# Three weight units of the first expert get places outside the ring

## What is computed

```python
logits = h @ w_router + b_router;  probs = softmax(logits, axis=-1)
vals, idx = lax.top_k(swapaxes(probs, 1, 2), 32)      # each expert takes 32 tokens
xe = h[idx]                                           # [16, 32, 1024]
a = einsum('becd,edf->becf', xe, w_gate_e)            # w_gate_e [16, 1024, 2048]
u = einsum('becd,edf->becf', xe, w_up_e)              # w_up_e   [16, 1024, 2048]
y = einsum('becf,efd->becd', silu(a) * u, w_down_e)   # w_down_e [16, 2048, 1024]
out = scatter_add(y * vals)
```

## Time and profile before

| | |
|---|---|
| median of three runs | 2342.8 us (2338.36 to 2347.49) |
| the profiled execution | 2340.59 us |
| its span, first to last instruction | 2338.8 us |
| mean granted TensorE clock | 0.871 |
| TensorE busy | 1814.7 us (78%) |
| VectorE, ScalarE busy | 830.5 us (36%), 632.7 us (27%) |
| moved by the DMA engines | 613.55 MB, 262 GB/s in the mean |

### The profile page before, as it was taken

The page is one execution under the profiler, slowest core; times in us unless marked ns, Lnnn a source line. Parts: engine busy times, 40 slices in busy tenths (PEclk is TensorE's granted clock), DMA queues, the critical chain, the costliest instruction groups (busy, mean ns, idle before and its releaser), DMA issues.

```text
span 2338.8 us, 33822 instructions
## 1 busy us (share of the span) xinstructions
PE 1814.7 (78%) x13686; PEld 1330.1 (57%) x13686; DVE 830.5 (36%) x1687; ACT 632.7 (27%) x1107; POOL 60.7 (3%) x94
## 2 busy tenths in 40 slices
PE   6999866656555556566555999969989997998998
PEld 4789721111111111111113989869979987988996
DVE  2364520000000000000004367754655544665553
ACT  1334300000000000000002256534633332643332
POOL 2000000000000000000000000100100000000000
PEclk7999978777888887877787899988989998998999
DMA  9886479999999999999997253243164543143540
GB/s 352 292 289 244 189 300 418 418 418 418 418 418 417 418 418 418 418 418 418 418 418 279 73 181 122 78 163 112 28 208 145 181 155 127 49 145 121 185 182 28
DMA packets 193908, 613.55 MB, mean 262 GB/s; under 512 B 8772, under 2 KB 62082, under 8 KB 161024
## 3 DMA queue, kind: packets, MB, share of 16 engines
q1 hardware_dynamic: 189856, 604.46, 67.1%
q0 software_dynamic: 3200, 7.14, 1.0%
q10 hardware_dynamic: 736, 0.38, 0.1%
HBM read 610.85 MB, written 5.03 MB: 263 GB/s over the span
## 4 chain that ended last, share of the span: by engine, by line
PE 52%; DMA 36%; DVE 4%; SPq 2%; issue 2%; DVEq 2%; ACT 1%; POOL 0%; POOLq 0%; ACTq 0%
PE psum L1247 51%; DMA ring<-in_w_down_e 18%; DMA ring<-in_w_up_e 17%; PE psum L1551 1%; DMA ring<-in_w_in 1%; SPq L696 1%; DVEq L1730 1%; DVE ring_r L646 1%; DVE xR L1712 0%; SPq L749 0%; DVEq L1713 0%; DVE xR L1714 0%; ACT arena L951 0%; PE psum L1327 0%; DVE mt L1725 0%
## 5 line engine op out<-in xcount | busy, mean ns | idle before, releaser
L1247 PE MATMUL psum<-ring,arena 128*32 128x512 f32 (+1 forms) x4316 | 544.1, 648 | 326.8 <-DMA ring<-in_w_up_e 135.9
L1247 PE MATMUL psum<-xR,ring_r 128*128 128x256 f32 x4416 | 576.6, 290 | 10.0 <-DVE xR L1714 7.0
L1247 PEld LDWEIGHTS psum<-xR,ring_r 128*128 128x128 f32 x4416 | 552.1, 196 | 22.3 <-issue 12.1
L1247 PEld LDWEIGHTS psum<-ring,arena 128*32 128x32 f32 x4316 | 155.5, 134 | 681.2 <-issue 225.6
L646 DVE TENSOR_TENSOR ring_r<-ring,ring_r 128x1024 fp32r<-128x1024 f32 (+2 forms) x332 | 377.3, 1171 | 280.3 <-ACT ring_r L637 280.0
L637 ACT CAST ring_r<-ring 128x1024 fp32r<-128x1024 f32 (+2 forms) x332 | 319.6, 1005 | 510.3 <-PE psum L1247 487.4
L1247 PE MATMUL psum<-arena 128*128 128x64 f32 (+8 forms) x1346 | 208.7, 363 | 21.1 <-ACT arena L1060 7.8
L1247 PE MATMUL psum<-ring_r,xR 128*128 128x256 f32 (+3 forms) x1488 | 208.8, 298 | 12.2 <-DVE xR L1714 9.9
L1247 PEld LDWEIGHTS psum<-ring_r,xR 128*128 128x128 f32 x1488 | 197.3, 208 | 17.7 <-DVE xR L1714 11.8
L1932 DVE TENSOR_TENSOR arena<-arena,psum 128x512 f32<-128x512 f32 x16 | 11.0, 687 | 493.1 <-PE psum L1247 493.1
L1247 PEld LDWEIGHTS psum<-arena 128*128 128x128 f32 (+5 forms) x1346 | 142.2, 185 | 56.8 <-issue 31.3
(11 more groups left out here) (199 smaller groups left out, 990.5 us busy)
## 6 DMA issues: line engine op xcount, KB each, us to landing
ring<-in_w_up_e SPq DMA_DIRECT2D x64, 2048.0 KB, 25.6
ring<-in_w_gate_e SPq DMA_DIRECT2D x64, 2048.0 KB, 23.7
ring<-in_w_down_e SPq DMA_DIRECT2D x64, 2048.0 KB, 26.9
ring<-in_w_in SPq DMA_DIRECT2D x30, 2048.0 KB, 11.9
ring<-in_w_ada SPq DMA_DIRECT2D x12, 2048.0 KB, 9.5
ring<-in_w_gate SPq DMA_DIRECT2D x22, 1024.0 KB, 5.4
ring<-in_w_up SPq DMA_DIRECT2D x22, 1024.0 KB, 8.1
ring<-in_w_down SPq DMA_DIRECT2D x10, 2048.0 KB, 7.9
```

The lines of the kernel that those rows point to most:

```text
L1247: return nc.tensor.matmul(o, l, r, start=s, stop=e)
```

## The change

Nine units of expert 0 are loaded before the experts begin, six in the ring as before and three outside: units 6 and 7 at the top of `arena` and unit 8 in the buffer `xR`. The two in `arena` are issued between the ring's third and fourth load, after waits for `z_done` and for two small stores of GpSimd that read tiles there; the one in `xR` is issued after the sixth. Unit 9 of expert 0 then goes to place 0, and all later units rotate from there (unit i to place (i - 3) mod 6). TensorE runs expert 0 written out and experts 1 to 15 in the loop; SyncE's loop runs over experts 1 to 14. For room, `wr` and `brow` stand below the top of the arena, the router's tiles overlie tiles of the expert loop, and GpSimd clears the second block's tiles only when nine units are used. The sum over all units, and what is computed, stays the same. Cut to its core:

```diff
+AHEAD = 3
-        xR = ctx.enter_context(nc.sbuf_tensor("xR", [P, 2 * KT * T], F32R))[:, :].rearrange("p (c k t) -> p c k t", c=2, k=KT)
+        x_moe, xR = twice("xR", 2 * KT * T)
+        xR = xR.rearrange("p (c k t) -> p c k t", c=2, k=KT)
...
-        wr = pl(KT * 32).rearrange("p (k e) -> p k e", k=KT)
-        brow = pl(NE)
+        top = Place(ARENA - KT * 32 - NE)
+        wr = top(KT * 32).rearrange("p (k e) -> p k e", k=KT)
+        brow = top(NE)
...
+        ahead_at = ARENA - KT * 32 - NE - 2 * SLOT
+        assert pm.at <= ahead_at
+        e_ahead = [arena[:, ahead_at:ahead_at + SLOT], arena[:, ahead_at + SLOT:ahead_at + 2 * SLOT], x_moe]
...
+        def moe_slot(e, i):
+            return (i if type(e) is int and e == 0 and i < RINGM else i - AHEAD) % RINGM
...
-            for i in [(N_MOE + j) % RING for j in range(RING)] + [RING]:
+            free = [(N_MOE + j) % RING for j in range(RING)]
+            for i in free + [RING]:
                 prev = max(n for n in range(N_MOE) if n % RING == i) if i < RING else N_MOE - 1
+                if i == free[3]:
+                    sp.wait_ge(z_done, 4)
+                    sp.wait_ge(rel_st, 16)
+                    sp.wait_ge(rel_na, 16 * 9)
+                    ahead_unit(0)
+                    ahead_unit(1)
                 sp.wait_ge(g_ready, LAST[prev] + 1)
-                expert_unit(0, i)
-            with sp.Fori(0, NE - 1) as e:
-                for i in range(RINGM, UPE):
-                    sp.wait_ge(e_unit, e * UPE + (i - RINGM + 1))
-                    expert_unit(e, i)
...
+                ring_unit(0, i)
+            ahead_unit(2)
...
+            for i in range(RINGM + AHEAD, UPE + AHEAD):
+                sp.wait_ge(e_unit, i - RINGM - AHEAD + 1)
+                ring_unit(i // UPE, i % UPE)
+            with sp.Fori(1, NE - 1) as e:
+                ring_units(e, AHEAD, UPE)
...
                 if n < RING:
-                    sp.wait_ge(e_unit, (NE - 1) * UPE + RINGM + n + 1)
+                    last = max(i for i in range(UPE) if moe_slot(1, i) == n)
+                    sp.wait_ge(e_unit, (NE - 1) * UPE + last + 1)
...
             pool.wait_ge(e_sel, 1)
+            pool.wait_ge(e_unit, RINGM + AHEAD)
...
-                pe.wait_ge(wm_ready[i % RINGM], e * (16 * UPE // RINGM) + 16 * (i // RINGM + 1))
-            with pe.Fori(0, NE) as e:
+                if type(e) is int and RINGM <= i < RINGM + AHEAD:
+                    pe.wait_ge(wx_ready[i - RINGM], 16)
+                    return e_ahead[i - RINGM]
...
+            expert(0)
+            with pe.Fori(1, NE) as e:
+                expert(e)
```

More of the change, by code:

```diff
@@ L348, in program @@
         csil = pl(KT * 32).rearrange("p (k n) -> p k n", k=KT)
-        wr = pl(KT * 32).rearrange("p (k e) -> p k e", k=KT)
-        brow = pl(NE)
+        top = Place(ARENA - KT * 32 - NE)
+        wr = top(KT * 32).rearrange("p (k e) -> p k e", k=KT)
+        brow = top(NE)
+        assert pl.at <= ARENA - KT * 32 - NE
         early = Place(ga_at)
@@ L370, in program @@
         xeT = pm(KT * CAP).rearrange("p (k c) -> p k c", k=KT)
+        routing = Place(pm.at)
         hT = pm(4 * P).rearrange("p (s n) -> p s n", s=4)
@@ L373, in program @@
         gu = pm(512)
+        lgp = routing(T)
+        work = routing(T)
+        mk = routing(T)
+        cnt = routing(T)
+        lg = routing(TT * NE).rearrange("p (t e) -> p t e", t=TT)
+        ex = routing(TT * NE).rearrange("p (t e) -> p t e", t=TT)
+        top8 = routing(8)
+        assert routing.at <= pm.at
         ysb = pm(T)
-        lgp = pm(T)
-        lg = pm(TT * NE).rearrange("p (t e) -> p t e", t=TT)
-        ex = pm(TT * NE).rearrange("p (t e) -> p t e", t=TT)
         prob = pm(TT * NE).rearrange("p (t e) -> p t e", t=TT)
[L379 to L382, removed]
         pp = pm((NE + 1) * 4).rearrange("p (e t c) -> p e t c", e=NE + 1, t=TT)
         cur = pm(4)
+        ahead_at = ARENA - KT * 32 - NE - 2 * SLOT
+        assert pm.at <= ahead_at
+        e_ahead = [arena[:, ahead_at:ahead_at + SLOT], arena[:, ahead_at + SLOT:ahead_at + 2 * SLOT], x_moe]
         p2 = Place(D)
@@ L485, in program @@
         wm_ready = [sem(f"wm_ready{i}") for i in range(RINGM)]
+        wx_ready = [sem(f"wx_ready{i}") for i in range(AHEAD)]
         w2_ready = [sem(f"w2_ready{i}") for i in range(RING)]
@@ L739, in _, with expert_unit @@
             wd = a["w_down_e"].rearrange("l e (k p) d -> p (l e k) d", p=P)
-            def expert_unit(e, i):
+            def expert_unit(e, i, d, landed_):
                 if i < 8:
@@ L744, in expert_unit @@
                     src = w[:, bass.ds(e * KT + 2 * (i % 4), 2), :]
-                    d = slot(i, RINGM).rearrange("p (k c) -> p k c", k=2)
+                    d = d.rearrange("p (k c) -> p k c", k=2)
                 else:
                     src = wd[:, bass.ds(e * (FE // P) + 4 * (i - 8), 4), :]
-                    d = slot(i, RINGM).rearrange("p (k c) -> p k c", k=4)
-                sp.dma_start(d, src).then_inc(wm_ready[i % RINGM], 16)
-            for i in [(N_MOE + j) % RING for j in range(RING)] + [RING]:
-                prev = max(n for n in range(N_MOE) if n % RING == i) if i < RING else N_MOE - 1
+                    d = d.rearrange("p (k c) -> p k c", k=4)
@@ new lines, in expert_unit, with ring_unit, ahead_unit @@
+                sp.dma_start(d, src).then_inc(landed_, 16)
+            def ring_unit(e, i):
+                n = moe_slot(e, i)
+                expert_unit(e, i, slot(n, RINGM), wm_ready[n])
+            def ahead_unit(j):
+                expert_unit(0, RINGM + j, e_ahead[j], wx_ready[j])
+            free = [(N_MOE + j) % RING for j in range(RING)]
+            for i in free + [RING]:
+                prev = max(n for n in range(N_MOE) if n % RING == i) if i < RING else N_MOE - 1
+                if i == free[3]:
[4 more added lines that the diff above has]
+                    ahead_unit(1)
@@ L754, in _, with ring_units @@
                 sp.wait_ge(g_ready, LAST[prev] + 1)
-                expert_unit(0, i)
-            with sp.Fori(0, NE - 1) as e:
-                for i in range(RINGM, UPE):
+                ring_unit(0, i)
+            ahead_unit(2)
+            def ring_units(e, lo, hi):
+                for i in range(lo, hi):
                     sp.wait_ge(e_unit, e * UPE + (i - RINGM + 1))
-                    expert_unit(e, i)
-                for i in range(RINGM):
-                    sp.wait_ge(e_unit, e * UPE + (i + RINGM + 1))
-                    expert_unit(e + 1, i)
@@ L763, in _ @@
-            for i in range(RINGM, UPE):
-                sp.wait_ge(e_unit, (NE - 1) * UPE + (i - RINGM + 1))
-                expert_unit(NE - 1, i)
+                    ring_unit(e, i)
+            for i in range(RINGM + AHEAD, UPE + AHEAD):
[3 more added lines that the diff above has]
+                ring_units(e, AHEAD, UPE)
+                for i in range(AHEAD):
+                    sp.wait_ge(e_unit, e * UPE + (UPE + i - RINGM + 1))
+                    ring_unit(e + 1, i)
@@ L767, in unit2 @@
+            ring_units(NE - 1, AHEAD, UPE)
             def unit2(name, *moves):
@@ L1446, in landed_e, with expert @@
             def landed_e(e, i):
-                pe.wait_ge(wm_ready[i % RINGM], e * (16 * UPE // RINGM) + 16 * (i // RINGM + 1))
-            with pe.Fori(0, NE) as e:
+                if type(e) is int and RINGM <= i < RINGM + AHEAD:
+                    pe.wait_ge(wx_ready[i - RINGM], 16)
+                    return e_ahead[i - RINGM]
+                n = moe_slot(e, i)
+                if type(e) is int:
+                    pe.wait_ge(wm_ready[n], 16 if i < RINGM else 32)
+                else:
+                    pe.wait_ge(wm_ready[n], e * 32 + 16 * ((i + RINGM - AHEAD) // RINGM))
+                return slot(n, RINGM)
+            def expert(e):
                 pe.wait_ge(e_sel, e + 1)
@@ L1468, in _ @@
                 for i in range(8):
-                    landed_e(e, i)
-                    w = slot(i, RINGM).rearrange("p (k c) -> p k c", k=2)
+                    w = landed_e(e, i).rearrange("p (k c) -> p k c", k=2)
                     for k in range(2):
@@ L1483, in _ @@
                 for q in range(4):
-                    landed_e(e, 8 + q)
-                    w = slot(8 + q, RINGM).rearrange("p (k c) -> p k c", k=4)
+                    w = landed_e(e, 8 + q).rearrange("p (k c) -> p k c", k=4)
                     for s in range(4):
```

## The result

| | before | after |
|---|---|---|
| median, 9 runs each | 2338.36 us (2332.96 to 2347.49) | 2325.86 us (2321.87 to 2332.09) |
| the profiled execution | 2340.59 us | 2332.09 us |
| its span | 2338.8 us | 2330.3 us |

The ratio is 0.9946, with a 95% interval from 0.9928 to 0.9963: 12.6 us less. The forecast was 15.1 us less, 2327.7 us; that the absolute time is only 1.8 us off owes something to the kernel before, whose median over nine runs is 4.4 us lower than over the three that the forecast started from.

A forecast was written before the change was run, and what follows sets the result against it. Expert-weight transfers at 418 GB/s bind about 400 to 1200 us, TensorE bounds the parts around them. Three unit periods, -15.07 us, plus 0 for all else, took 2342.8 to 2327.7 us; range 2320 to 2336.

The forecast's parts named there:

- Step 1: Full transfer stretch of the experts: three units leave it, everything behind comes 3 x 5.022 = 15.07 us sooner, the whole gain.
- Step 2: Queue before the experts: the three early loads fit in the hole there and cost 0; unhidden, their 15 us again.
- Step 3: Start of expert 0: units run without the load queue emptying, the seventh load comes 16 us in time; cost 0.
- Step 4: Expert 0 written out on TensorE, SyncE's loop peeled: longer program, bounds 0 and 1 us, taken as 0.
- Step 5: GpSimd's four memsets move behind unit 8's use, near 323 us: gain of 0 to 0.9 us, taken as 0.
- Step 6: End of the experts: second block's first loads wait for later units; delay up to 3.4 us free, taken as 0.
- rival A: Second block's start: queue runs dry and ScalarE's squares wait, losing some 4 to 9 us of the gain; 12%.
- B: Start of the experts' stream: it begins three units' time later, so no gain, 2342.8 us; 5%.
- Rival C: TensorE after the experts: reduced clock loses 15 us or more, kernel slower than before, 2358 us for 30 us lost; 3%.
- the 5 us either way: Full-busy TensorE stretches at reduced clock after the last unit: they can grow or shrink, allowed 5 us each way.
- C's sign: Stretch from the last unit to the end: over 1094 us + 3 would show the clock loss.
- a last unit later than 1232: Last expert: last unit forecast to start at 1230.0 us; later than 1232 would mean Step 1 or Step 3 wrong.

The follow-up runs named there:

- the first comparison: Changed kernel against the kernel before, nine runs each: ratio 0.9946 (0.9928 to 0.9963), 12.6 us less.
- that of the second: Changed kernel, unedited, measured again against the kernel before, beside the earliest follow-up experiments: ratio 0.9934 (0.9918 to 0.9949), 15.4 us less.

## Why the prediction was right

Step 1, three periods of 5.022 us: shown. The stretch from the first looped load to the last unit's start is 15.2 us shorter (938.2 to 923.0), 0.1 us more than the term, and two units ahead give 10.0 us. The moved rate is 418 GB/s after as before. The share of about 358 GB/s that the Trainium skill gives for one core (DMA: Bandwidth & Descriptors, Specifications), by which the term would have been 17.6 us, is not borne out by these traces, in which one core runs alone.

Step 2, the early loads are hidden: shown, more widely than argued. Even issued last, all three are in place in time.

Step 3, the stream stays full at its start: shown by the same piece. The interval between the last up unit and unit 8 was 2.14 us (2.15 forecast). The forecast had TensorE meet the landings in expert 1 or 2; it did in expert 1.

Step 4, the longer program: no cost that the runs could measure with no unit ahead (ratio 0.9996, 0.9985 to 1.0007). The instruction queue grew by four packets:

```profile
q8 instruction: 80, 1.31, 0.2%
```

Step 5, the memsets: no cost, and no gain either (TensorE's wait ahead of unit 0 is 1.02 us, 1.10 before). Step 6, the second block's loads: ScalarE's slack was 3.25 us against 3.39, and the 9.2 us for a load from an empty queue came out as 9.3. What was mis-sized there is the price of overrunning it, on which rival A rests: it counts every us beyond the slack in full, and in the profile with the later loads 1.65 of 3.9 us reached TensorE.

Rivals A and B did not come about: the squares do not stand behind a landing, and the first looped load goes out at once with unit 0's release. Rival C, the clock, did not come about either: the piece from the last unit to the end was 1088 to 1096 us over all profiles, with no relation to the kernel to be seen. In the changed kernel it was 1093.9, 1096.3 and 1089.1 us, within the 5 us either way that the forecast gave it, and C's sign, over 1097 us, showed in no profile. The two comparisons came out at 12.6 and 15.4 us; their intervals overlap, and both hold 15.1. The 2.5 us by which the first falls short lie within this noise.

What the prediction left out is the front. It gave no term to the 300 us ahead of the experts, since nothing in them changes; they moved by up to 8 us between profiles with the copies in their old place. One of its own signs of being wrong, a last unit later than 1232, did show: it began at 1236.38 in the first profile (and at 1230.63 and 1230.49 in the two others of this kernel). The sign was put as a time from the start of the program, and so it took the front's 6.6 us for a fault of step 1 or 3. The first looped load, forecast at 306.8, went out at 313.42 for the same reason. That the whole came out well inside the range is in part luck, since front and tail each vary by half of the gain or more.

**Open.** Whether part of the front's wait belongs to the change. It was 3.25 to 5.71 us in five profiles without units ahead and 4.84 to 10.40 in six with them, though neither set issues other work there. Expert 0 began at 301.85 to 303.38 in the five and at 303.67 to 309.72 in the six, 3.6 us later in the mean. Chance can do this in eleven profiles, but it is not the likelier reading, and no experiment tells why. It goes through the load beside the two copies, since the wait becomes 2.67 us in both kernels once these are moved. The run times don't settle it. With 3.6 us lost the gain would be 11.5 us: that lies inside the interval of the first comparison (8.7 to 16.8 us), just outside that of the second (11.9 to 19.2) and outside that with the loads issued late (13.6 to 20.6).

## What to carry to other kernels

Where transfers bind a stretch and a hole lies ahead of it, the gain of loading more in the hole is the bytes moved over the rate of the full stretch (here 5.02 us for each 2 MB), and a buffer that is dead at that time will do as a place; it can be measured inside one profile, from the first load of the rotation to the last landing, where it stands out of the noise of the whole. Compare a profile piece by piece before a difference of a few us is put down to a change. A forecast's sign of being wrong is better put as the length of a piece than as a time from the start, which carries the noise of everything ahead of it. And look at what is issued beside a load on the critical path: here copies that are wanted much later were cheaper behind the experts. A place for them in the hole was not tried.

## What was not expected

Two copies of together 3.8 MB, wanted only by the later blocks, made a 2 MB load beside them take 21 to 27 us instead of 10.2, and the wait behind it 3.3 to 10.4 us instead of 2.67; with them moved the kernel before takes 2.8 us less. The use of unit 0 takes 2.0 or 3.4 to 3.9 us by the clock at that moment, and since it releases the stream behind it the whole experts' stretch begins up to 1.9 us earlier or later. Twenty transposes ahead of it brought the full clock, but to a stretch in which TensorE had next to nothing to do, and the gather behind it ran at the half one.
